# The attention's probability blocks turned by VectorE and a copy through DRAM in place of TensorE transposes

## What is computed

```python
h = rms_norm(x, pre_norm)
proj = h @ w_in                      # q, k, v, gate_a, u_b, v_b, gate_b, mg_a, mg_b
o_a = sliding_window_attention(q, k, v, sinks, rel_bias)   # 16 query heads of 64, 2 k/v heads
y_a = (o_a * silu(gate_a)) @ w_branch_a
o_b = spatial_gating(gelu(u_b), gelu(v_b), ...)
y_b = (o_b * silu(gate_b)) @ w_branch_b
merged = sigmoid(mg_a) * y_a + sigmoid(mg_b) * y_b
x = x + rms_norm(merged @ w_out, post_norm)
```

## Time and profile before

| | |
|---|---|
| three runs, us | 908.32, 908.79, 909.49 |
| median, us | 908.79 |
| span of the profiled execution, us | 907.8 |
| TensorE busy, us (share of the span) | 898.6 (99%) |
| VectorE, ScalarE, GpSimd busy | 71%, 54%, 55% |
| TensorE's granted clock, share of full speed | 0.999 |
| DMA: packets, MB | 126591, 122.50 |

### The profile page before, as it was taken

One profiled execution on the slowest core, in us unless ns is written; L12 is line 12 of the kernel. 1 busy time (PEld: TensorE's weight loads), 2 busy tenths in 40 slices (PEclk: granted clock), 3 DMA queues, 4 the chain that ended last, 5 costly groups with the idle time before them and its releaser, 6 DMA issues.

```text
span 907.8 us, 12649 instructions
## 1 busy us (share of the span) xinstructions
PE 898.6 (99%) x4332; PEld 754.5 (83%) x4332; DVE 641.5 (71%) x1135; ACT 490.6 (54%) x948; POOL 498.1 (55%) x395
## 2 busy tenths in 40 slices
PE   9999999999999999999999999999999999999997
PEld 7878888888888888888888888888888888888886
DVE  6866695565656464656565678688689878989968
ACT  6554254766756675756566763334443434534563
POOL 3574335778686868595868675445542252043236
PEclk9999999999999999999999999999999999999999
DMA  8888864323223244323223243534289550435004
GB/s 288 212 189 234 261 201 113 128 82 93 71 82 94 82 129 139 94 70 94 82 82 94 82 139 104 186 116 119 67 286 338 186 209 1 139 112 213 1 1 185
DMA packets 126591, 122.50 MB, mean 135 GB/s; under 512 B 23208, under 2 KB 95936, under 8 KB 126272
## 3 DMA queue, kind: packets, MB, share of 16 engines
q1 hardware_dynamic: 124288, 118.27, 41.0%
q10 hardware_dynamic: 2240, 3.43, 1.2%
HBM read 89.68 MB, written 35.15 MB: 137 GB/s over the span
## 4 chain that ended last, share of the span: by engine, by line
PE 95%; DVE 2%; SPq 1%; DMA 1%; issue 0%; ACT 0%; DVEq 0%; POOLq 0%; POOL 0%; ACTq 0%
PE acc L967 51%; PE acc L1147 11%; PE ps_m L1147 7%; PE ps_t L1147 7%; PE acc L820 6%; PE ps_t L984 3%; PE ps_m L1014 3%; PE acc L910 2%; PE ps_t L994 2%; SPq L478 1%; DMA x_both<-in_x 1%; DVE sums L1910 0%; PE ps_t L850 0%; PE ps_m L850 0%; DMA ht_d<-sums 0%
## 5 line engine op out<-in xcount | busy, mean ns | idle before, releaser
L967 PE MATMUL acc<-mv,w_hi 128*128 128x512 f32 x1344 | 353.2, 393 | 0.0
L967 PEld LDWEIGHTS acc<-mv,w_hi 128*128 128x128 f32 x1344 | 245.2, 188 | 44.9
L967 PE MATMUL acc<-mv,w_lo 128*128 128x512 f32 x672 | 181.2, 391 | 0.0
L967 PEld LDWEIGHTS acc<-mv,w_lo 128*128 128x128 f32 x672 | 126.3, 188 | 28.2
L1747 POOL TENSOR_TENSOR w_lo<-sums,w_hi 128x1024 fp32r<-128x1024 f32 x48 | 116.3, 2425 | 45.7 <-ACT w_hi L1312 38.3
L1747 POOL TENSOR_TENSOR w_lo<-raw,w_hi 128x1024 fp32r<-128x1024 f32 (+1 forms) x48 | 94.6, 1972 | 42.1 <-ACT w_hi L1305 36.1
L1147 PE MATMUL acc<-right,left 128*128 128x512 f32 x432 | 98.7, 390 | 0.0
L1147 PEld LDWEIGHTS acc<-right,left 128*128 128x128 f32 x432 | 81.1, 188 | 17.1 <-DVE left L2127 0.4
L1792 POOL TENSOR_SCALAR_AFFINE_SELECT pt_prev<-pt_pack 128x512 fp32r<-128x512 f32 x64 | 41.7, 651 | 85.8 <-DVE pt_pack L2063 85.8
L1514 ACT ACTIVATE prob<-neg_s,neg_max 128x129 f32<-128x129 f32 x128 | 50.6, 397 | 68.6 <-DVE neg_max L2072 68.5
L820 PE MATMUL acc<-mv 128*128 128x512 f32 x288 | 69.3, 394 | 0.5 <-POOL mv L1697 0.5
(11 more groups left out here) (282 smaller groups left out, 1681.9 us busy)
## 6 DMA issues: line engine op xcount, KB each, us to landing
raw<-in_w_in SPq DMA_DIRECT2D x56, 512.0 KB, 4.0
ht_d<-sums SPq DMA_DIRECT2D x8, 512.0 KB, 4.0
mix_d<-mix_b SPq DMA_DIRECT2D x8, 512.0 KB, 3.7
ga_d<-gate SPq DMA_DIRECT2D x16, 256.0 KB, 2.0
tb<-tb_d SPq DMA_DIRECT2D x4, 1024.0 KB, 5.2
ub<-mix_d SPq DMA_DIRECT2D x7, 512.0 KB, 3.5
gb_d<-ub SPq DMA_DIRECT2D x7, 512.0 KB, 2.6
x_both<-in_x SPq DMA_DIRECT2D x6, 512.0 KB, 6.4
```

What stands on the lines that cost most here:

```text
L967: ins = nc.tensor.matmul(bank, (w_lo if y == 2 else w_hi)[:, left + k * P:left + (k + 1) * P], right[:, (OPW if y == 1 else 0) + k * HALF: ...
```

## The change

`transpose_p` is gone from TensorE. For each query block (64 in all, 8 to a pair, two heads in each) the work is now this, with the step in which each engine has it in its order:

- step b + 1, VectorE: after the scores of that step, `nc.vector.transpose(w, w)` on each head's 128 by 128 probabilities. It transposes each square of 32 by 32 within itself; the squares stay where they are.
- step b + 1, SyncE: one DMA of 128 KB writes the block of both heads to `prob_d` in DRAM, in pieces of 512 bytes.
- step b + 2, SyncE: it waits until that has landed (`prob_out`) and issues four DMAs, one for each group of 32 key rows. Each reads 32 KB in pieces of 128 bytes (one row of one square) and puts the squares in their places in `turned_in`.
- step b + 3, VectorE: at the end of its attention work, not before the scores as before, it waits for all four (`prob_back`) and splits `turned_in` into `pt_pack`. The source is now in SBUF and was in PSUM.

Three things go with it to make room. `neg_s` holds one query block, not two, and `o_tmp` is one buffer, not two, so that ScalarE waits for GpSimd's gating of one group before it writes the next. The weight loads of column blocks before 16 stand one step later in SyncE's order. ScalarE's `exps` wait until the buffer of three blocks ago has been written to DRAM. Some semaphores are merged with others that count in the same order. The weight work, the scores and the values' products are the same.

```diff
@@ -372,10 +377,13 @@
 
             return slice(blk % 4 * 2 + h, blk % 4 * 2 + h + 1)
 
-        def neg_w(blk, h):
-
-            c = (blk % 2 * 2 + h) * SINK_W
-            return neg_s[:, c:c + SINK_W]
+        def squares(s):
+            return prob[s % 3][:, :].rearrange("p (h j) -> p h j", h=2)[:, :, 0:P]
+        def neg_w(h):
+            return neg_s[:, h * SINK_W:(h + 1) * SINK_W]
 
         bmat = ub[:, 3072:4096]
...
                              bass.AP(skew_d, p * (2 * P * BIAS_ROW) + (P - 1),
                                      [[BIAS_ROW - 1, P], [P * BIAS_ROW, 2], [1, 2 * P]])).then_inc(bias_in, 16)
 
+            def prob_squares_back(s):
+
+                sp.wait_ge(prob_out[s % 2], 16 * (s // 2 + 1))
+                if s >= 2:
+                    sp.wait_ge(ptl_ok, s - 1)
+                for g in range(4):
+                    sp.dma_start(turned_in[s % 2][32 * g:32 * (g + 1), :].rearrange("a (h q b) -> a h q b", h=2, q=4),
+                                 prob_d[s, :, :].rearrange("(q a) (h g b) -> g a h q b", q=4, h=2, g=4)[g]
+                                 ).then_inc(prob_back[s % 2], 16)
+
             def attend(p, k):
+                if 2 <= k < 10:
+                    prob_squares_back(8 * p + k - 2)
+                if 1 <= k < 9:
+                    s = 8 * p + k - 1
+                    sp.wait_ge(turn_ok, s + 1)
+                    sp.dma_start(prob_d[s, :, :].rearrange("p (h j) -> p h j", h=2), squares(s)).then_inc(prob_out[s % 2], 16)
                 if k == 8 and p + 1 < HEAD_PAIRS:
                     load_bias(p + 1)
...
@@ -740,9 +764,9 @@
                     if n == 0 and s == 6:
                         sp.wait_ge(vlo_ok, 2)
                         sp.dma_start(v_d[:, :], v_tmp[:, :].bitcast(i32)).then_inc(v_out, 16)
-                    if s == 4:
+                    if s == (5 if n < FIRST_U else 4):
                         load_pair(n + 2, 0)
-                    if s == 5:
+                    if s == (6 if n < FIRST_U else 5):
                         load_pair(n + 2, 1)
                     if n == FIRST_U and s == 2:
...
@@ -985,16 +1009,6 @@
                                                kbuf[:, kc + lo:kc + 256], start=a, stop=not a, skip_group_check=True)
                 ins.then_inc(scores_ok, 1)
 
-            def transpose_p(p, blk):
-                s = 8 * p + blk
-                pe.wait_ge(prob_ok, s + 1)
-                if s:
-                    pe.wait_ge(ptl_ok, s)
-                for h in range(2):
-                    ins = nc.tensor.transpose(ps_p[:, h * P:(h + 1) * P], prob[blk % 3][:, h * SINK_W:h * SINK_W + P],
-                                              ident[:, :])
-                ins.then_inc(pt_done, 1)
-
             def values(p, blk):
                 pe.wait_ge(pt_ok, 8 * p + blk + 1)
...
                 for h in range(2):
-                    ins = nc.scalar.activation(prob[blk % 3][:, h * SINK_W:(h + 1) * SINK_W], neg_w(blk, h), ACT.Exp, scale=-1.0,
+                    ins = nc.scalar.activation(prob[s % 3][:, h * SINK_W:(h + 1) * SINK_W], neg_w(h), ACT.Exp, scale=-1.0,
                                                bias=neg_max[:, head(blk, h)], accum_out=row_sum[:, head(blk, h)])
                 ins.then_inc(exp_ok, 1)
 
             def norm(p, blk):
                 act.wait_ge(inv_ok, 8 * p + blk + 1)
                 for h in range(2):
-                    w = prob[blk % 3][:, h * SINK_W:h * SINK_W + P]
+                    w = prob[(8 * p + blk) % 3][:, h * SINK_W:h * SINK_W + P]
                     ins = nc.scalar.activation(w, w, ACT.Copy, scale=inv_den[:, head(blk, h)])
                 ins.then_inc(prob_ok, 1)
...
                     gg = 4 * p + g
                     act.wait_ge(values_ok, 2 * gg + 2)
-                    if gg >= 2:
-                        act.wait_ge(og_ok, gg - 1)
+                    if gg:
+                        act.wait_ge(og_ok, gg)
                     o = ps_m[:, (g % 2) * 512:(g % 2 + 1) * 512]
-                    nc.scalar.activation(o_tmp[g % 2][0:64, :], o[64:128, 0:256], ACT.Copy)
-                    nc.scalar.activation(o_tmp[g % 2][64:128, :], o[0:64, 256:512], ACT.Copy).then_inc(otmp_ok, 1)
+                    nc.scalar.activation(o_tmp[0:64, :], o[64:128, 0:256], ACT.Copy)
+                    nc.scalar.activation(o_tmp[64:128, :], o[0:64, 256:512], ACT.Copy).then_inc(otmp_ok, 1)
 
             def after(n, s):
...
-                    nc.gpsimd.tensor_scalar(neg_s[:, :].rearrange("p (b h j) -> p b h j", b=2, h=2)[:, :, :, P],
-                                            sink_b[:, None, 2 * p:2 * p + 2].to_broadcast([P, 2, 2]), 1.0, 1.0, ALU.mult,
-                                            ALU.mult).then_inc(sink_ok, 1)
+                    nc.gpsimd.tensor_scalar(neg_s[:, :].rearrange("p (h j) -> p h j", h=2)[:, :, P],
+                                            sink_b[:, 2 * p:2 * p + 2], 1.0, 1.0, ALU.mult, ALU.mult).then_inc(sink_ok, 1)
                 if 3 <= k < 11:
...
-                    s = 8 * p + k - 3
-                    dve.wait_ge(pt_done, s + 1)
-                    if s == 0:
-                        dve.wait_ge(v_out, 16)
-                    if s >= 2:
-                        dve.wait_ge(values_ok, s - 1)
-                    pack = pt_pack[(k - 3) % 2]
-                    own.link(nc.vector.tensor_copy(pack[:, 0:256], ps_p))
-                    nc.vector.tensor_tensor(pack[:, 256:512], ps_p, pack[:, 0:256].bitcast(f32), ALU.subtract).then_inc(ptl_ok, 1)
                 if k < 8:
                     dve.wait_ge(scores_ok, 8 * p + k + 1)
-                    if 8 * p + k >= 2:
-                        dve.wait_ge(exp_ok, 8 * p + k - 1)
+                    if 8 * p + k:
+                        dve.wait_ge(exp_ok, 8 * p + k)
                     if k > 0:
                         own.link(nc.vector.copy_predicated(blocks(ps_s)[:, :, 1, :], before_i, blocks(ps_s)[:, :, 0, :]))
                     for h in range(2):
                         bias = h * 256 + (0 if k else P)
                         ins = nc.vector.tensor_tensor_reduce(
-                            out=neg_w(k, h)[:, 0:P], in0=ps_s[:, h * 256 + P:(h + 1) * 256], in1=bias_t[:, bias:bias + P],
+                            out=neg_w(h)[:, 0:P], in0=ps_s[:, h * 256 + P:(h + 1) * 256], in1=bias_t[:, bias:bias + P],
                             scale=-HEAD_DIM ** -0.5, scalar=sink_b[:, 2 * p + h:2 * p + h + 1], op0=ALU.add, op1=ALU.min,
                             accum_out=neg_max[:, head(k, h)])
                     ins.then_inc(scores_used, 1)
+                if 1 <= k < 9:
+                    s = 8 * p + k - 1
+                    dve.wait_ge(prob_ok, s + 1)
+                    for h in range(2):
+                        w = prob[s % 3][:, h * SINK_W:h * SINK_W + P]
+                        ins = nc.vector.transpose(w, w)
+                    ins.then_inc(turn_ok, 1)
+                if 3 <= k < 11:
+                    s = 8 * p + k - 3
+                    dve.wait_ge(prob_back[s % 2], 64 * (s // 2 + 1))
+                    if s == 0:
+                        dve.wait_ge(v_out, 16)
+                    if s >= 2:
+                        dve.wait_ge(values_ok, s - 1)
+                    pack = pt_pack[s % 2]
+                    own.link(nc.vector.tensor_copy(pack[:, 0:256], turned_in[s % 2][:, :]))
+                    nc.vector.tensor_tensor(pack[:, 256:512], turned_in[s % 2][:, :], pack[:, 0:256].bitcast(f32),
+                                            ALU.subtract).then_inc(ptl_ok, 1)
                 if k >= 7 and k % 2:
                     g = (k - 7) // 2
                     gg = 4 * p + g
```

More of the change, by code:

```diff
@@ L36 @@
 ACT_H, ACT_WSH = (1, 3), 2
+POOL_FRONT = 5
 Q_COL = 0
@@ L211, in build @@
                 prob = [sb(f"prob{b}", [P, 2 * SINK_W], f32, s1) for b in range(3)]
-                o_tmp = [sb(f"o_tmp{b}", [P, 256], f32, s1) for b in range(2)]
+                o_tmp = sb("o_tmp", [P, 256], f32, s1)
+                turned_in = [sb(f"turned_in{b}", [P, 256], f32, s1) for b in range(2)]
                 gate = [sb(f"gate{b}", [P, SEQ], f32, s1) for b in range(2)]
@@ L294, in build @@
             sem("scores_ok"), sem("scores_used"), sem("exp_ok"), sem("inv_ok"), sem("prob_ok"))
-        pt_done, ptl_ok, pt_ok, values_ok = sem("pt_done"), sem("ptl_ok"), sem("pt_ok"), sem("values_ok")
+        turn_ok, ptl_ok, pt_ok, values_ok = sem("turn_ok"), sem("ptl_ok"), sem("pt_ok"), sem("values_ok")
+        prob_out = [sem(f"prob_out{b}") for b in range(2)]
+        prob_back = [sem(f"prob_back{b}") for b in range(2)]
         otmp_ok, oadd_ok, og_ok = sem("otmp_ok"), sem("oadd_ok"), sem("og_ok")
```

55 lines of the change are left out of this document (26 added, 29 removed).

## The result

The changed kernel takes 976.0 us in the median against 909.1 us for the kernel before: a ratio of 1.074, 95% interval 1.072 to 1.075, 67 us slower. The profiled execution spans 974.1 us against 907.8, at a granted clock of 0.994.

The account below looks back on a forecast made before the run. TensorE, 99% busy, bounds the kernel; after the change SyncE's round, 30.1 + 6.4 + 1.5 + 14.5 = 52.5 us a pair against 47.6, adds 36 us to 907.8: 945 us, 8 in 10 for 901 to 983.

Parts of the forecast that it names:

- What goes: TensorE: two transposes a block leave, saving 0.21 us a block, 1.7 us a pair, 13 us for all 64.
- VectorE: Two transposes at 0.3 us add 0.6 us a block; split keeps two 0.42 us operations; 70% busy, not a bound.
- SyncE's cycle c: SyncE, each block: write landing plus four read issues cannot overlap, c = w + 4i = 4.3 us, the deciding term.
- w: SyncE: time from the write's issue to its landing, taken as 2.0 us, bounds 1.4 and 3.2.
- i: SyncE: one read's issue with its gap, taken as 0.58 us, between 0.46 for plain loads and 0.71 for squares.
- The end of the round: Pair's end: last write's landing, three issues, last read's landing 6.4 us; split and masked copy 1.5; old border chain 14.5.
- Who waits: TensorE waits first for `scores_used` while VectorE stands before a split, then for `pt_ok` of the last blocks.
- plain price: Rival, SyncE's reads: i = 0.46 makes the round 49.0 us, 10 us more, 919; chance 0.17 for 909 to 925.
- all hidden: Rival, SyncE: reads issue in 0.33 us, round 42 to 46 us, TensorE never waits, 896; chance 0.2.
- Held by GpSimd: Rival, VectorE's split from SBUF: GpSimd delays each pair's last split 2.2 us, 16 us more, 961; within the 0.55 case.
- The Trainium skill's estimate: DMA about 2.0 us plus bytes at 436 GB/s: write 2.3, last read 2.1 us, pair 1.8 us more, near 958.

Follow-up runs that it names:

- every_other: Changed kernel with only blocks 0, 2, 4 and 6 of a pair turned by VectorE through DRAM, the others transposed by TensorE: 902.0 us, ratio 0.992.
- one_read: Changed kernel with one read of the whole block in its own rows for the four of squares, output not attention's: 901.8 us, ratio 0.992.
- turn_thrice: Changed kernel with each of VectorE's 128x128 transposes done three times in place, waits on its own queue between: 988.6 us, ratio 1.0885.
- five_issues: Changed kernel with the fourth read of each block split by head into two, five reads with the same bytes: 1002.8 us, ratio 1.1035.
- two_queues: Changed kernel with the reads of squares 2 and 3 issued from ScalarE's queue, 0 and 1 from SyncE: 932.2 us, ratio 1.025.
- plain_reads: Changed kernel with each of the four reads taking 32 whole rows, squares left unplaced, output not attention's: 926.7 us, ratio 1.020.
- write_first: Changed kernel with SyncE issuing the write of block b+1 ahead of the reads of block b: 956.3 us, ratio 1.052.
- late_split: write_first with VectorE's split and GpSimd's masked copy one attention step later, TensorE's steps kept: 967.4 us, ratio 1.063.
- late_split_two_q: Changed kernel with write ahead of reads, reads on SyncE and ScalarE, and split and masked copy one step later: 975.4 us, ratio 1.073.
- two_q_wfirst: Changed kernel with write_first's order and the reads of squares 2 and 3 from ScalarE's queue: 927.5 us, ratio 1.020.
- late_values: late_split_two_q with TensorE's products with the values one attention step later as well: 963.4 us, ratio 1.059.

## Why the prediction was right in kind and short in size

- **What goes**: 0.21 us a block, right (every_other; one_read has 1.2 us for eight, where full cover would give 1.7).
- **VectorE**: 0.3 us a transpose, measured 0.29 (page of groups: 268/290/314 ns). The copy of the split from SBUF took 0.29 where 0.42 was priced. Right, and no bound (turn_thrice).
- **SyncE's cycle c** was the right term, five_issues and two_queues show it, and it was sized 4.3 us. Seven cycles took 34.64 us, 4.95 each. Summed over the seven, 16.6 us passed from a write's issue to the first read, 2.38 each against w = 2.0, one of them 3.23 and the rest 2.2 to 2.3; and 18.0 us on the issues, 0.64 a read against i = 0.58. That is +2.6 and +1.8 us a pair: the terms that failed. i lies halfway between the middle that I took and the 0.71 of the squares; a plain read with its gap has 0.46. So the shape weighed more than I let it; how much the quarter of the pieces took off is not parted from it. For w the nearest row was 0.2 too low, and a stretched landing a pair was not in the sum.
- **The end of the round**: landing, three issues and last landing 6.6 us (6.4 forecast). From there to the first turned block 14.8 us, 16.0 forecast. Of the 1.2 us, 0.9 lie behind the new scores: VectorE reads the second scores 1.8 us after the first (500.41, 502.23) and not 2.8 as before, where it waited 0.5 us for TensorE. The stretch up to the new scores was 0.4 us shorter.
- Together 52.5 + 4.5 + 0.2 - 1.2 = 56.0 us, as measured. That is 8.4 us over a pair of before (8.3 in the mean) and not 4.9; eight times 8.3 is 66 us of the measured 67, against 36.
- **Who waits**: for the products with the values, yes, but 24.5 us of that for `ps_m` to be freed by `o_tmp`'s addition, a wait that the prediction did not name; for the scores, 4.3 us in all, which the prediction had put first.
- **The rivals**: "plain price" and "all hidden" hold for other shapes, as plain_reads and one_read show, with 927 and 902 us. For plain_reads the sum gives 919 at i = 0.46; its regular cycles are 3.9 us, but in the pair from 417.76 two of seven took 4.7 and 4.9, by a stretched issue and a stretched landing, which makes most of the rest. "Held by GpSimd" did not come in the changed kernel (L2093 never over 0.427 us), but it did in variants whose split falls at another time: 1.47 us once in every pair of write_first, and 2.5 us in seven pairs of late_split.
- The Trainium skill's estimate (DMA: Bandwidth & Descriptors, Anatomy of one DMA), 2.3 us for the write and 2.1 for a read, stands against medians of 2.2 and 2.3 here. Its 958 us was nearer than 945, and still short, since it puts other values on w and the last landing only and leaves i at 0.58.

Why late_split_two_q lost 48 us against two_q_wfirst is shown only by chains of waits; no run took the third loop away. Left open too is what stretches a landing. In the changed kernel seven of the 64 writes took 2.8 to 3.3 us to the first read and the others under 2.4. In six of the seven one packet of an instruction queue (q8 or q14 of the page) passes in that time, as in five of the other 57. A weight load issued at 469.63 did not stretch the landing under way since 468.27 (2.23 us). In plain_reads the write of 438.03 landed after 3.2 us with the DMA engines 97% busy. Neither was tried by itself.

## What to carry to other kernels

Price a round trip of a block through DRAM as latency per block in the queue that issues it: landing plus every issue, four of squares being as dear as the landing. If that sum is over the step in which the block comes, the queue falls behind however empty the DMA engines are; the trip for every other block only made the same idea a gain, and one plain issue does so only where no square has to change its place, as in one_read. And when one wait is taken out of such a ring, look in each in-order queue for the next loop before counting the gain: here the runs took out one and then a second, and the trace of late_values shows a third.

## What the runs showed of the hardware

- The issue of a read on SyncE, in the median: a plain one 0.32 us alone (one_read), 0.30 as the first of four and 0.42 behind another (plain_reads); one of squares (32 partitions by 8 pieces of 128 bytes) 0.56 as the first and 0.61 behind another. Two reads with half as many pieces behind three of squares: 0.60 and 0.43 (five_issues).
- A read of 32 KB landed in 1.8 us in whole rows (plain_reads) and in 2.3 us in squares, in the median.
- VectorE's copy with rounding of 128x256 took 0.29 us from SBUF and 0.42 from PSUM.
- VectorE's split of two SBUF operands, 0.43 us, took up to 2.5 us when GpSimd was at work. In late_split it was over 0.8 us 14 times in 64, each time with an operation of GpSimd on two SBUF operands running beside it; one stands in the chain:

```profile
411.75 2.51 DVE pt_pack L2093
```
